# Identity products on TensorE in the router's idle stretches of a one-core hybrid layer step

## The reference, cut to what matters

```python
mixed, final_state = token_mixer(h, p, init_state)             # ends with  merged @ p['w_out']
x = layer_norm(DN_ALPHA * x + gate1 * mixed, ln1_g, ln1_b)
h = layer_norm(x) * (1.0 + scale2) + shift2                    # h2 below
x = layer_norm(DN_ALPHA * x + gate2 * hier_moe(h, p), ln2_g, ln2_b)

def hier_moe(h, p):
    lg = h @ w_rg + b_rg                       # 4 groups
    g_sel = argmax(lg)                         # one group for each token
    le_sel = (h @ w_re + b_re)[g_sel]          # its 8 experts
    top_v, top_i = top_k(le_sel, 2)
    gate = softmax(top_v) * max(softmax(lg))   # spread over the 32 experts
    hid = silu(h @ w_e1) * (h @ w_e3)          # each expert: 1024 -> 256
    return sum over experts of (hid * gate) @ w_e2
```

## Time and profile before

| | us |
|---|---|
| median of 3 runs | 1444.11 (1443.04 to 1444.88) |
| the profiled execution | 1445.52 |
| its span, first to last instruction | 1443.7 |
| PE busy / share of the span | 1295.9 / 90% |
| DVE busy / share | 559.0 / 39% |
| ACT busy / share | 291.7 / 20% |
| mean granted clock of TensorE | 0.946 |

### The profile page before, as it was taken

One profiled execution on the slowest core, in us unless ns is written; L12 is line 12 of the kernel. 1 busy time (PEld: TensorE's weight loads), 2 busy tenths in 40 slices (PEclk: granted clock), 3 DMA queues, 4 the chain that ended last, 5 costly groups with the idle time before them and its releaser, 6 DMA issues. The chain is left out here.

```text
span 1443.7 us, 15342 instructions
## 1 busy us (share of the span) xinstructions
PE 1295.9 (90%) x5936; PEld 768.0 (53%) x5936; DVE 559.0 (39%) x1288; ACT 291.7 (20%) x595; POOL 70.7 (5%) x123
## 2 busy tenths in 40 slices
PE   3899999788989899989999999999998399599765
PEld 1455555464566778657767655555446234244222
DVE  5230576568312333433544551111286611111117
ACT  2201354254033323411111110000001011111112
POOL 0000000000000000000000000000200112122100
PEclk9999999898999899999999999999998599899887
DMA  9533134210201102011111112821515689999945
GB/s 374 201 124 138 59 117 175 88 16 22 95 6 35 64 7 64 1 67 52 50 39 44 44 47 85 255 66 44 227 76 214 241 326 419 421 419 420 413 173 204
DMA packets 58748, 214.07 MB, mean 148 GB/s; under 512 B 20878, under 2 KB 29646, under 8 KB 42030
## 3 DMA queue, kind: packets, MB, share of 16 engines
q1 hardware_dynamic: 53342, 201.48, 36.9%
q0 software_dynamic: 5184, 10.50, 1.9%
q10 hardware_dynamic: 144, 1.05, 0.2%
HBM read 203.65 MB, written 17.74 MB: 153 GB/s over the span
## 5 line engine op out<-in xcount | busy, mean ns | idle before, releaser
L501 PE MATMUL bank<-hT,ring 128*128 128x512 f32 x320 | 165.3, 598 | 0.0
L2660 PE MATMUL bank<-ew,xgT 128*64 128x512 f32 (+2 forms) x544 | 133.9, 636 | 26.8 <-issue 24.8
L1647 PE MATMUL bank<-hT,w_ab 128*128 128x512 f32 x256 | 131.1, 594 | 0.8 <-issue 0.8
L2660 PEld LDWEIGHTS bank<-ew,xgT 128*64 128x64 f32 (+2 forms) x544 | 48.0, 147 | 109.9 <-issue 109.0
L502 PEld LDWEIGHTS bank<-hT,ring 128*128 128x128 f32 x320 | 60.8, 190 | 76.5 <-issue 76.5
L928 PE MATMUL bank<-hT,ring 128*128 128x512 f32 x192 | 98.6, 595 | 2.2 <-DVE yA L1445 2.2
L1648 PEld LDWEIGHTS bank<-hT,w_ab 128*128 128x128 f32 x256 | 48.6, 190 | 61.2 <-issue 61.2
L2084 PE MATMUL bank<-w_out,mT 128*128 128x512 f32 x160 | 70.9, 604 | 2.2 <-PEq L1580 2.2
L2675 PE MATMUL bank<-ew,hidT 128*64 128x512 f32 (+2 forms) x272 | 67.0, 623 | 3.5 <-DMA ew<-in_experts 2.8
L2806 DVE SCALAR_TENSOR_TENSOR uh<-uh,bank 128x256 f32<-128x256 f32 x18 | 7.6, 421 | 153.9 <-ACT uh L2745 153.9
L1762 PE MATMUL bank<-hT,w_c 128*128 128x512 f32 x128 | 65.5, 594 | 0.0
(11 more groups left out here) (455 smaller groups left out, 2060.8 us busy)
## 6 DMA issues: line engine op xcount, KB each, us to landing
ew<-in_experts SPq DMA_DIRECT2D x96, 1024.0 KB, 21.9
ring<-in_blocks SPq DMA_DIRECT2D x10, 2048.0 KB, 8.3
mhalf<-in_mods SPq DMA_DIRECT2D x16, 1024.0 KB, 5.0
w_ab<-in_merge SPq DMA_DIRECT2D x16, 768.0 KB, 4.4
mstage<-in_mods SPq DMA_DIRECT2D x3, 2048.0 KB, 18.0
w_c<-in_merge SPq DMA_DIRECT2D x8, 768.0 KB, 4.4
yt<-expert_rows SPq DMA_DIRECT2D x5, 1024.0 KB, 11.8
w_out<-in_w_out SPq DMA_DIRECT2D x1, 4096.0 KB, 12.0
```

Source lines behind the costliest of these rows:

```text
L501: pe.matmul(lat[:, :], w, hT[:, k, P:T], start=(k == 0), stop=(k == KD - 1))
L1647: pe.matmul(bank[5][:, :], w[:, k, :], hT[:, k, P:T], start=(k == 0), stop=(k == KD - 1))
L2660: mm = pe.matmul(bank[2 + n % 2][hs, :], xgT[:, n % 2, k, hs], ew1[w][k // 4][:, 512 * (k % 4):512 * (k % 4) + 512], start=(k == 0), stop= ...
```

## The change

A function `filler(pe, n)` is added, which issues n products of the identity with itself (128 x 128 by 128 columns, fp32) into the first 128 columns of bank 7. It waits for nothing, signals nothing, and nobody reads the bank. It is called in five places of TensorE's queue: in "out", turn i = 6, 10 products ahead of logits(3) and 3 behind turn(4); in "route" 22 at the block's start, ahead of the wait for `mall`, 48 between the rank sums and the wait for `rhs`, and 24 behind the table, at the block's end.

```diff
+    def filler(pe, n):
+
+        for _ in range(n):
+            pe.matmul(bank[7][:, 0:P], ident, ident, start=True, stop=True)
@@ out, TensorE, the loop over i @@
                 if i == 3:
                     pe.wait_ge(got8, 32)
+                if i == NT + 1:
+                    filler(pe, 10)
                 if i >= 3:
                     logits(i - 3)
                 if 0 <= i - 2 < NT:
                     turn(i - 2)
+                if i == NT + 1:
+                    filler(pe, 3)
@@ route, TensorE @@
+            filler(pe, 22)
             pe.wait_ge(v9.sem, v9.after("mall"))
...
             mm.then_inc(p9.step("rank"), 1)
+            filler(pe, 48)
             pe.wait_ge(v9.sem, v9.after("rhs2"))
...
             mm.then_inc(p9.step("tab"), 1)
+            filler(pe, 24)
```

## The result

The changed kernel takes 1433.27 us (median of 4, 1432.89 to 1434.53) against 1444.38 us for the kernel before (4 runs, 1443.04 to 1444.88): ratio 0.9929, 95% interval 0.9917 to 0.9942. That is 10.3 us by the ratio and 11.1 by the medians. The forecast was 1436.9 us in a range of 1435.0 to 1440.2: faster, as said, but by more than said. The profiled execution took 1434.53 us, its span is 1432.7. One execution of a later kernel (e12) took 2320.37 us at a mean granted clock of 0.554; its ratio leaves it out.

A forecast was written before the change was run, and what follows sets the result against it. One serial chain on a half-clocked TensorE, ending in unit 0's ffn1, was taken to delay the DMA-full load stream. Gains 2.8 + 1.05 + 1.1 + 3.65 = 8.6 us, from 1445.5, gave 1436.9 us, range 1435.0 to 1440.2.

The forecast's parts named there:

- Bound and chain: Serial chain from logits(3) to unit 0's ffn1 starts the load stream; a microsecond gained ahead is gained in all.
- The rival that the stream swallows the gain: The DMA stream is bound from elsewhere, so the time stays at 1444.1 to 1445.5 us; chance 0.04.
- Price of a product: One identity product is two records, each about 0.112 us at full clock, about 0.22 at the low one.
- A: Last tile in "out": with 10 and 3 products, logits(3), turn(4) and logits(4) run at full clock; gain 2.8 us.
- B: 22 products ahead of the rank sums in "route" make these warm, VectorE becomes the bound; gain 1.05 us.
- C: 48 products ahead of the table make it warm, and `tab` loses its idle 1.10 us; gain 1.1 us.
- D: 24 products while the gathers run; transposes and unit 0's ffn1 then run at full clock; gain 3.65 us.
- the first rival: Clock falls in the gap before the table; table and 24 products begin cold; 6.0 us gained, 1439.5 us; chance 0.36.
- the stream as long as before: Expected sign: the load stream behind unit 0's ffn1 keeps its length, set by its bytes; 217 us at full share.
- the rest: First expert load of the stream to the end of the span: forecast gain 0.
- The base: Gain subtracted from the profiled execution's 1445.5 us; the median before, 1444.11, is 1.4 lower, which was not taken off.
- The slow rival: Identity products don't hold or bring back the clock; cold groups delay critical steps, some 20 us, 1466 us; chance 0.06.

The follow-up runs named there:

- e12: Kernel before, plus 17 products behind TensorE's last unit and 23 at the start of final: 1442.91 us against 1443.68, ratio 0.9991.
- e2: Changed kernel without the 10 and 3 products around the last tile: 1440.38 us, ratio 0.9974 to the kernel before.
- e3: Changed kernel without the 24 products behind the table: 1437.89 us, ratio 0.9957 to the kernel before.
- e15: Changed kernel with 40 instead of 24 products behind the table: 1437.01 us, ratio 0.9961 to the kernel before.
- e4: Changed kernel with only the 24 products behind the table left in: 1440.42 us, ratio 0.9978 to the kernel before.
- e9: Kernel before, plus 10 products ahead of ffn2 of the last unit but one: 1443.63 us against 1443.68, ratio 0.9998.

## Why the prediction was wrong

- Bound and chain: right. The stream of loads starts behind unit 0's ffn1, is full for 217 us as before (share 1.00, 411 GB/s), and what the chain gains comes through. The clock is at 0.50 inside it (1238 to 1251.2 us before, 1226.6 to 1243.3 in the change), 3.5 us longer in the change, and that costs nothing: from the first load to the ffn1 of the last unit but one it is 202.6 us in both. The rival that the stream swallows the gain is out.
- Price of a product: right. 96 records in 10.96 us is 0.114 each. The 81 ns of the Trainium skill (TensorE: Matmul & The Clock Gate, Back-to-back issue gap) don't hold for these fp32 records, which took 114 ns each.
- A: 3.08 for 2.8. The error is small: logits(4) started 3.51 us behind logits(3), where the sum had 3.72, and took 1.87 us.
- B: 1.17 for 1.05. C: 1.17 for 1.1; `tab` lost its wait. D: 3.66 for 3.65.
- The 24 products: the first rival came, in two of three profiles, in a milder form. The clock fell late in the table, which still ended in time for `tab`; the products took 7.08 us and the transposes came 1.1 us late, where I had put 1.5 and all of C. In the third profile it did not fall.
- The step that failed: "the stream as long as before", and with it the claim that all of the gain lies before the first load. The stream is nearly, within 0.6 us (first load to that ffn2: 226.3 before, 226.3, 225.8 and 225.7 in the change's three profiles); what follows it isn't. In each of three profiles the rest, which the sum had at a gain of nothing, is about 2 us shorter, most of it in ffn2 of the last unit but one, 3.64 for 5.34 us. I had that gap before me and used it only as evidence on the clock, not as a place where a shift of everything ahead could turn a fall into none.
- The base: I subtracted from the profiled execution's 1445.52 and refused to take off its 1.4 us, as luck "in just this stretch". The luck was elsewhere: logits(3) began at 1107.63, the latest of three profiles, with 1105.44 the earliest; the 1.15 us that the profiles of the table above differ by there is luck and no work of the change.
- Together: 1436.9, less 1.15 for the base, less 1.87 for the rest, plus the 0.6 by which the chain gave less than forecast, gives 1434.5, the time of the profiled execution. The median, 1433.27, lies 1.3 us lower, as the median before lay 1.1 below its profiled execution: a sum made from one execution sat that much too high from the start.
- The slow rival (products don't hold the clock) is out, but e2 shows its mechanism in small: a group that begins cold ends late.

What stays open: why the change puts the cold part of that ffn1 where it lasts longer. That the position of the stretch against the clock's changes decides it fits the two groups and their order by the length of the chain, e3's short rest just beyond e15's long one included; but no run moved the position alone, so the cause is argued from that order and not shown.

## What to carry to other kernels

Idle TensorE ahead of a critical short step is worth filling if the products fit the idle time at full clock and begin while the clock is still up; close the chain of gaps from its first, since a group begun cold ends late and gives back part or all of what it saves (e4's 24 products kept 1.5 of 3.7 us, e2's 22 lost 0.5). Count what a shift does to every later gap whose length is near those at which the clock fell in one profile and held in another (here 1.1 to 3.2 us): 2 of 10 us came from one such gap, some 230 us further on. Take the base for the sum from several profiles, or from a landmark just ahead of the change to the end.

## What the runs showed of the hardware

- Ahead of the same ffn2, in sixteen profiles, the clock fell behind 2.7 to 3.2 us of idle and held behind 1.1 to 2.1. It also fell in the table behind only 1.9 us of idle (1130.17 to 1132.08; 0.50 in 1134.5 to 1137.5), when the work that followed was 84-column products paced by VectorE, in two of three profiles of the change. Of all eight profiles with 48 products there and 1.7 to 1.9 us of idle behind them it fell in six; in the three with 54 products and 0.56 us of idle it held.
- 48 records begun at the low clock, or with it fallen just before, took 6.78 to 7.42 us, against 5.56 at full clock; 44 took 7.59 against 5.15.
- Holding the clock in one gap moved its rise in a later one: in e9, one profile, the first sum of final took 6.4 instead of 5.7 us.
